# Eight of twelve slices of the modulation matmul are computed inside the prompt's attention; the attention's order of work is changed; pads move the rings in SBUF

## The reference

```python
mod = silu(c) @ w_mod + b_mod            # (1024) @ (1024 x 6144), per sequence
sh1, sc1, gt1, sh2, sc2, gt2 = split(mod, 6)
h = x * (1 + sc1) + sh1
x = LN1(ALPHA * x + (1 + gt1) * mixer(h))   # h @ w_in, attention A and B, RMS norms, @ w_out
h = x * (1 + sc2) + sh2
x = LN2(ALPHA * x + (1 + gt2) * PEER(h))    # 8 heads, top 16 of 128 x 128 experts each
```

## Time and profile before

| | us |
|---|---|
| median of three runs | 4421.73 (4414.55 to 4424.63) |
| the profiled execution, its own time | 4414.03 |
| its span | 4412.2 |
| PE busy | 3550.2, 80% |
| DVE busy | 3054.6, 69% |
| POOL busy | 2662.0, 60% |
| ACT busy | 793.1, 18% |
| mean granted clock of PE | 0.907 of full |

### The profile page before, as it was taken

One profiled execution on the slowest core, in us unless ns is written; L12 is line 12 of the kernel. 1 busy time (PEld: TensorE's weight loads), 2 busy tenths in 40 slices (PEclk: granted clock), 3 DMA queues, 4 the chain that ended last, 5 costly groups with the idle time before them and its releaser, 6 DMA issues. The chain is left out here.

```text
span 4412.2 us, 36769 instructions
## 1 busy us (share of the span) xinstructions
PE 3550.2 (80%) x10274; PEld 1775.6 (40%) x10274; DVE 3054.6 (69%) x7027; ACT 793.1 (18%) x1597; POOL 2662.0 (60%) x2632
## 2 busy tenths in 40 slices
PE   8885599577777774688888888888888888888887
PEld 1444355354554542333333333343333333333333
DVE  1126777688777875877777777777777777777774
ACT  0141111244444441101101101101111111111100
POOL 0000056465555552777777777777777777777775
PEclk9878799688778887899999999999999999999999
DMA  8320489877777776999999999999999999999998
GB/s 326 114 115 24 157 285 313 316 258 265 258 262 270 274 264 257 388 420 419 416 420 414 413 414 412 416 416 411 411 420 412 414 420 414 411 420 413 411 416 324
DMA packets 436081, 1500.23 MB, mean 340 GB/s; under 512 B 47317, under 2 KB 67797, under 8 KB 433621
## 3 DMA queue, kind: packets, MB, share of 16 engines
q0 software_dynamic: 368640, 1342.34, 77.4%
q1 hardware_dynamic: 51928, 128.60, 7.8%
q10 hardware_dynamic: 15360, 27.53, 1.7%
HBM read 1464.96 MB, written 33.33 MB: 340 GB/s over the span
## 5 line engine op out<-in xcount | busy, mean ns | idle before, releaser
L1679 PE MATMUL e_acc<-e_up,e_diag 128*128 128x512 f32 x4096 | 1951.7, 622 | 330.0 <-DMA e_up<-in_up,e_idx 225.5
L1582 DVE CUSTOM_DVE_ANT_0 e_down<-e_down,e_h_ps 128x1024 f32<-128x1024 f32 x1024 | 1244.0, 1219 | 666.4 <-DMA e_down<-in_down,e_idx 664.6
L1679 PEld LDWEIGHTS e_acc<-e_up,e_diag 128*128 128x128 f32 x4096 | 763.1, 196 | 1478.5 <-issue 821.4
L1509 POOL DMA_INDIRECT e_down<-in_down,e_idx x1024 | 993.6, 970 | 355.5 <-issue 223.3
L1509 POOL DMA_INDIRECT e_up<-in_up,e_idx x1024 | 1001.4, 978 | 332.1 <-issue 271.8
L272 POOL DMA_INDIRECT w_in_a<-in_up,a_idx_up x192 | 220.3, 1147 | 275.5 <-DVE sums L303 216.0
L546 PE MATMUL p_acc<-w_in_a,p_h1t 128*128 128x512 f32 x640 | 282.5, 600 | 45.0 <-DVEq L467 45.0
L1052 PE MATMUL a_turn<-ident_sb,a_prob 128*128 128x128 f32 x784 | 154.6, 340 | 169.7 <-ACT a_prob_t L796 163.2
L303 DVE SCALAR_TENSOR_TENSOR sums<-w_in_a,a_wgt,sums 128x1024 f32<-128x1024 f32 x192 | 263.0, 1370 | 29.8 <-DMA w_in_a<-in_up,a_idx_up 23.2
L1222 ACT ACTIVATE e_gate_e<-e_best,e_neg_b 128x16 f32<-128x16 f32 x64 | 19.7, 307 | 1461.7 <-DVEq L1275 1461.7
L264 POOL DMA_INDIRECT w_in_a<-in_down,a_idx_down x192 | 221.5, 1154 | 79.5 <-issue 50.6
(11 more groups left out here) (206 smaller groups left out, 3471.6 us busy)
## 6 DMA issues: line engine op xcount, KB each, us to landing
wm<-in_w_mod SPq DMA_DIRECT2D x12, 2048.0 KB, 8.7
w_in_a<-in_w_in SPq DMA_DIRECT2D x4, 4096.0 KB, 19.1
e_down<-in_down,e_idx POOLq DMA_INDIRECT x1024, 9.5
e_up<-in_up,e_idx POOLq DMA_INDIRECT x1024, 9.5
w_in_a<-in_w_query SPq DMA_DIRECT2D x1, 8192.0 KB, 28.7
p_xt<-in_x_t SPq DMA_DIRECT2D x10, 512.0 KB, 3.4
scratch_qt<-p_qk_t ACTq DMA_DIRECT2D x10, 512.0 KB, 2.8
a_q_t<-scratch_qt SPq DMA_DIRECT2D x20, 256.0 KB, 6.8
```

What stands on the lines that cost most here:

```text
L1509: pool.indirect_dma_start(ring, None, table, bass.IndirectOffsetOnAxis(ap=index, axis=0)).then_inc(landed, 16)
L1582: nc.vector.tensor_tensor_reduce(row, row, h2_ps[:], 1.0, 0.0, ALU.mult, ALU.add, dots[n % 2][:, s:s + 1]).then_inc(dotted, 1)
L1679: mm = nc.tensor.matmul(acc[t % 2][:, c * 512:(c + 1) * 512], diag[n % 2][:, s, :], up[:, r % RING, c * 512:(c + 1) * 512], start=n % PH = ...
```

## The change

The block `modulation` computes 4 of the 12 slices, those that the projection needs. Its 1 is now added with the bias, in one instruction. SP issues the `w_in` loads right behind the four slices, and the stores of zeros behind these. The other 8 slices are loaded in `attention(0)` into `w_in_a` (free by then), and PE multiplies half a slice (four matmuls) in each of the 16 steps of the first tile. The results lie in the unused halves of the score banks. `mod_rows` is stored in two parts, and the prompt's `rows` are loaded in its second tile.

In both attentions the merge goes behind the head's denominator and side dot rows, the transposes of the merged rows from step 2 to 3, `mix` from steps 3 to 6 to steps 4 to 7, and its two halves have a bank and a wait of their own (`mix_ps`). They are read in steps 7 and 8. In the layer norm two fused instructions take the place of three. ACT does the side rows' `Gelu` ahead of the head's exponential. POOL's `tail` of the sample goes from step 11 to 12, and the transposes of h2 from 12 to 14.

`silu` (64 bytes of a partition) moves into the outer allocation, with a pad of 160 bytes behind it; there are pads of 128 bytes in `projection(1)` and of 32 bytes in `experts`.

```diff
@@ modulation
-    CH, BUFS = 512, 4
-    NCH = 6 * D // CH
+    CH = MOD_CH                      # 512
+    NCH = MOD_FIRST                  # 4; MOD_REST = 8
@@ sync
-            with sp.Fori(1, NCH // BUFS) as r:
-                for b in range(BUFS):
-                    sp.wait_ge(row_done, (r - 1) * BUFS + b + 1)
-                    hold(sp)
-                    sp.dma_start(wm[b][:], ...)
+            w_in = io["w_in"].rearrange("(c p) n -> p c n", p=P)
+            sp.dma_start(keep["w_in_a"][:, :, 0:VA], w_in[:, :, 0:VA]).then_inc(keep["w_in_first"], 16)
+            sp.dma_start(keep["w_in_a"][:, :, VA:], w_in[:, :, VA:2048]).then_inc(keep["w_in_loaded"], 16)
+            sp.dma_start(keep["w_in_b"][:], w_in[:, :, 2048:INW]).then_inc(keep["w_in_loaded"], 16)
             sp.wait_ge(zeroed, 1)
             for slot in (0, 3, 4, 13):
                 sp.dma_start(io["kb"][slot], zeros[:]).then_inc(stored, 16)
                 sp.dma_start(io["vb"][slot], zeros[:]).then_inc(stored, 16)
-            (the three w_in loads)
-            sp.wait_ge(mod_ready, 1)
-            sp.dma_start(io["mod_rows"], mod[:, 2 * D:6 * D]).then_inc(stored, 16)
-            sp.wait_ge(stored, 16 * 9)
+            sp.wait_ge(stored, 16 * 8)
@@ attention
-    M_AT, MIX_AT, READ_AT, LN_AT, H2_AT = 2, (3, 4, 5, 6), 7, 9, 12
+    M_AT, TURN_AT, MIX_AT, READ_AT, LN_AT, TAIL_AT, H2_AT = 2, 3, ((4, 5), (6, 7)), (7, 8), 9, 12, 14
+            mod = sb("mod", [2, 4 * D])
+            wm = [keep["w_in_a"][:, :, b * MOD_CH:(b + 1) * MOD_CH] for b in range(4)]
+        mix_ps = [score[1][:, 512:1024], turn[:, 4:8, :].rearrange("p k q -> p (k q)")]
+            rows_ps = [score[b][0:2, 512:1024] for b in range(2)]
@@ sync, load
+                if not first and not side:
+                    wait(row_added, 2 + ROWS + MOD_REST * 3 // 4)
+                    sp.dma_start(io["mod_rows"][:, 0:3 * D], mod[:, 0:3 * D]).then_inc(mod_stored, 16)
+                    sp.wait_ge(mod_stored, STORES + 16)
+                    load_rows()
...
+                    sp.dma_start(mod[:], io["b_mod"][2 * D:6 * D].partition_broadcast(2)).then_inc(bias_in, 16)
+                    for n in range(4):
+                        load_mod(n)
                 (ln, gn, w_out)
+                    for n in range(4, MOD_REST):
+                        sp.wait_ge(row_done, ROWS + n - 3)
+                        load_mod(n)
@@ vector
             def layer_norm(j):
-                chain.then(nc.vector.tensor_scalar(x2[:], z, mv[:, 0:1], lr[:, 2:3], ALU.subtract, ALU.mult))
-                chain.then(nc.vector.tensor_tensor(x2[:], x2[:], ln[:, 0, :], ALU.mult))
-                nc.vector.tensor_tensor(x2[:], x2[:], ln[:, 1, :], ALU.add).then_inc(x2_ready, 1)
+                chain(nc.vector.scalar_tensor_tensor(out=x2[:], in0=z, scalar=mv[:, 0:1], in1=ln[:, 0, :],
+                                                     op0=ALU.subtract, op1=ALU.mult))
+                ...
+                nc.vector.scalar_tensor_tensor(out=x2[:], in0=x2[:], scalar=lr[:, 2:3], in1=ln[:, 1, :],
+                                               op0=ALU.mult, op1=ALU.add).then_inc(x2_ready, 1)
+            def add_bias(n):
+                at = slice(n * MOD_CH, (n + 1) * MOD_CH)
+                dve.wait_ge(bias_in, SMALL + 16)
+                dve.wait_ge(row_done, ROWS + n + 1)
+                nc.vector.scalar_tensor_tensor(out=mod[:, at], in0=rows_ps[n % 2],
+                                               scalar=0.0 if D <= n * MOD_CH < 2 * D else 1.0,
+                                               in1=mod[:, at], op0=ALU.add, op1=ALU.add).then_inc(row_added, 1)
@@ vector, body
                     mask(i, h)
-                    if not first and h == M_AT:
-                        merge(i - 1)
-                    if not first and h == READ_AT:
-                        mix(i - 1)
+                    if not side and first and h >= 2 and h % 2 == 0:
+                        add_bias(h // 2 - 1)
+                    if not first and h == READ_AT[1]:
+                        read_mix(i - 1, 1)
                     (denominator, dot rows)
+                    if not first and h == M_AT:
+                        merge(i - 1)
                     (weigh, add rows)
+                    if not first and h == READ_AT[0]:
+                        read_mix(i - 1, 0)
+                    if not first and h == READ_AT[1]:
+                        residual(i - 1)
@@ tensor
+            def modulate(n, half):
+                (waits for wm slice n, and for the bank's last reader)
+                for c in range(half * DC // 2, (half + 1) * DC // 2):
+                    mm = nc.tensor.matmul(rows_ps[n % 2], keep["silu"][:, 2 * c:2 * c + 2], wm[n % 4][:, c, :],
+                                          start=(c == 0), stop=(c == DC - 1))
+                if half:
+                    mm.then_inc(row_done, 1)
             (body, after sum_values)
+                    if not side and first:
+                        modulate(h // 2, h % 2)
@@ program
+        keep["silu"] = sb("silu", [P, 2 * DC])
+        sb("line_pad", [P, 40])
```

More of the change, by code:

```diff
@@ L170, in _ @@
             nc.vector.tensor_tensor(silu[:], c_t[:], sig[:], ALU.mult).then_inc(silu_ready, 1)
[L171 to L176 removed]
+            for j in range(NCH):
+                dve.wait_ge(row_done, j + 1)
+                nc.vector.scalar_tensor_tensor(out=mod[:, j * CH:(j + 1) * CH], in0=rows[j % 2][0:2, :],
+                                               scalar=1.0 if j >= NCH // 2 else 0.0,
+                                               in1=bias[:, j * CH:(j + 1) * CH], op0=ALU.add, op1=ALU.add
+                                               ).then_inc(row_copied, 1)
             dve.wait_ge(row_copied, 2 + NCH)
[L178 to L179 removed]
             dve.sem_inc(mod_ready, 1)
@@ L766, in body @@
                             side_rows.take_down(pool, chain, 0, i + 1)
-                    if not first and h == H2_AT - 1:
+                    if not first and h == TAIL_AT:
                         tail(i - 1)
@@ L829, in body @@
                     g = i * HEADS + h
+                    if side and h % 8 == 0 and not (first and h == 0):
+                        side_rows.activate(act, *chunk_before(i, h))
                     act.wait_ge(masked, g + 3)
@@ L848, in body @@
                         square(i - 1)
-                    if not first and h == READ_AT + 1:
+                    if not first and h == READ_AT[1] + 1:
                         root(i - 1)
@@ L945, in weigh_w_out, with read_mix, residual @@
                                         ALU.mult).then_inc(keep["w_out_weighed"], 1)
-            def mix(j):
-                dve.wait_ge(mixed, j + 1)
-                for c in range(2):
-                    chain(nc.vector.tensor_tensor(z[:, c * 512:(c + 1) * 512], score[c][:, 512:1024],
-                                                  rows[:, 0, c * 512:(c + 1) * 512], ALU.mult))
-                chain.wait()
+            def read_mix(j, c):
+                dve.wait_ge(mixed, j * 2 + c + 1)
+                chain.then(nc.vector.tensor_tensor(z[:, c * 512:(c + 1) * 512], mix_ps[c],
+                                                   rows[:, 0, c * 512:(c + 1) * 512], ALU.mult))
                 dve.sem_inc(mix_read, 1)
+            def residual(j):
                 dve.wait_ge(x_sem, (j + 1) * 16)
@@ L1013, in _ @@
             add_rows(0, 8)
-            mix(last)
+            for c in range(2):
+                read_mix(last, c)
+            residual(last)
             add_rows(8, 10)
@@ L1103, in body @@
                     if h + 1 < HEADS:
-                        if not first and h + 1 == BH:
-                            pe.wait_ge(mix_read, i)
+                        if not first and h == BH:
+                            pe.wait_ge(mix_read, i * 2 - 1)
                         scores(i, h + 1)
@@ L1108, in body @@
                         scores(i + 1, 0)
-                    if not first and h == M_AT + 1:
+                    if not first and h == TURN_AT + 1:
                         pe.wait_ge(merged_copied, i)
+                    if not first and h == BH:
+                        pe.wait_ge(mix_read, i * 2)
                     if not first and h == H2_AT + 1:
@@ L1115, in body @@
                         sum_values(*before(i, h, 1))
-                    if not first and h == M_AT:
+                    if not side and first:
+                        modulate(h // 2, h % 2)
+                    if not first and h == TURN_AT:
                         turn_merged(i - 1, g0 + h + 2)
-                    if not first and h in MIX_AT:
-                        mix(i - 1, (h - MIX_AT[0],))
+                    for c in range(2):
+                        if not first and h in MIX_AT[c]:
+                            part = MIX_AT[c].index(h)
+                            mix(i - 1, c, part * DC // 2, (part + 1) * DC // 2)
```

(3 more changed lines are left out.)

117 lines of the change are left out of this document (62 added, 55 removed).

## The result

The changed kernel took 4381.1 us (median of 4 runs, 4377.4 to 4383.7), the kernel before 4418.4 us beside it: a ratio of 0.9924, 95% interval 0.9903 to 0.9944. It is faster by 37 us by the medians, and by 33 by the ratio, where 67 were forecast: the time lies inside the range, but nearer to rival B (4385) than to the forecast (4347). A second set of runs gave 0.9926 (0.9908 to 0.9944). The profiled execution took 4383.3 us, 30.7 less than that of before, and its windows by stage answer to the earlier trace rows.

A forecast was written before the change was run, and what follows sets the result against it. Bounds taken: DMA in experts (2697 of 4412 us), PE in modulation and attention(0)'s first tile (half clock), DVE with its waits in attention(1). -48 + 37 - 8 - 49 = -68 us from 4414.03; forecast 4347, range 4305 to 4390.

The forecast's parts named there:

- rival B: In attention(1) the waits only move: a gain of 1 to 2 us a tile, kernel at 4385; chance 0.14.
- They shrink: Attention(1): DVE's waits for PE, 11.0 us a tile, do not vanish but lose 4.3 through later, split reads.
- I charge nothing more: Attention(1): h2 stores moved to step 15, beside SP's query, mask and x loads, cost nothing beyond the lower bound of 2.
- Modulation, -48 forecast: Front block: four slices instead of twelve, ending near 54.5 us instead of 102.94; gain 48 us, between 44 and 57.
- First tile, +37 forecast: Prompt's first tile in attention(0): eight slices added on PE, 88 us against 51.4; loss 37, between 33 and 41.
- Rival C: Prompt's first tile: the clock does not rise, 164 us instead of 88, kernel at 4426; chance 0.04.
- Second tile and tail, -8 forecast: Attention(0): warm start 3 us, reordered reads and layer norm 3, tail 2; gain 8, bounds 3 and 13.
- the tile starts at full clock, so I take 3 us: Attention(0)'s second tile: full clock instead of half for two or three heads, ACT's chain covering part; gain 3 us.
- Attention(1), -49 forecast: Seven reordered tiles: 8.8 us a tile by terms, taken as 7; gain 49 us, bounds 14 and 84.
- The waits for the root and in `weigh` go: Attention(1): DVE's waits for the square root, 1.4 us a tile, and of `weigh`, 2.3, go through the new order.
- Pads, 0 forecast: Rings put on 256-byte boundaries: experts unchanged, having that already; attention(1) 0 us, bounds 0 and 2.
- The rows show half a per cent between the two stages: Pads: 413 GB/s off a boundary in attention(1) against 415 on one in experts, set against up to 6% by the skill.

The follow-up runs named there:

- h2 at 13, second sum: Changed kernel with h2 turned at step 13, first four slices asked for ahead of k_t, last Gelu ahead of last squares on ACT: 4354.8 us, 0.9877.
- h2 at 12, first sum: Changed kernel with h2 at step 12, early slices, and in attention(1)'s end Gelu ahead of squares, four rows added before the merge: 4369.9 us, 0.9905.

## Why the prediction was wrong, and where it was right

The gain was forecast at 67 us and is 33 to 37. The step that failed is that of `attention(1)`, -49 forecast and -22.2 measured: "They shrink", of the waits for PE (11.0 to 6.7 us a tile forecast, 10.9 measured), the waits for ACT that were to go and stayed at 3.8, and "I charge nothing more" for the moved h2 stores, which cost 17.6 us after the last tile. Next comes the second tile of `attention(0)` (-8 forecast, +3.6 measured). With the first tile 5.6 us over its term and `modulation` 4.9 us better than its own, the terms miss by 39 us together, and by 27 of them in one stage. That the time still fell into the range is due to the width of the range.

**Modulation, -48 forecast, -52.9 measured.** Right in mechanism, mis-sized by the rate: 17.8 MB at 408 GB/s with 3 us ahead and 3 behind is 50, the number that the prediction worked out and passed over.

**First tile, +37 forecast, +42.6 measured** (134.63 to 228.41, and 0.2 us at the stage's start). Two terms were too small, by little each. A half slice takes 3.53 us from its first matmul to the next instruction (151.86 to 155.39) where 3.43 was taken, and a head's other matmuls 1.71 in the mean where half of the old head, 1.61, was taken: the shapes of the score, the turn and the values fall from 1.65, 0.90 and 1.49 us to 0.91, 0.55 and 0.83 between the two clocks, which is 0.55 to 0.61 and not 0.5. Over fifteen heads that is 3.0 us. The first head costs 2.7 more, mostly the stall of 5.42 us where 3 stood; asking for the slices first took it down to 2.70. Rival C (clock at 1.2 GHz through the tile) did not come: 1.00 from 189.8 to 228.4.

**Second tile and tail, -8 forecast, +3.6 measured** (120.6 us from 228.41, 117.0 from 238.54). The step "the tile starts at full clock, so I take 3 us" failed in its sign. What is late next is ACT's chain, it doesn't get faster, and a faster PE only waits longer for it and loses its clock. DVE's masks of heads 1, 8 and 15 of that tile, us from the start of the stage, show what each part did:

```
                            head 1   to head 8   to head 15   to the end
before                        59.2        38.8         21.9         54.5
old order, split, pads       101.5        41.6         22.9         53.7
new order, slices in front    59.2        36.4         25.8         57.8
changed                      101.1        36.1         25.8         57.7
changed, h2 at 12            101.2        36.1         28.9         51.8
```

With the old order the split makes the heads up to 8 slower by 2.8 us; with the new one it makes no difference (36.4 and 36.1), and they are 2.7 faster than before. The heads behind them are 3.9 slower in the new order, where second read, residual and layer norm stand in a row on DVE. h2 at 14 costs 5.9 in the tail against 12, and saves 3.1 ahead of it.

**Attention(1), -49 forecast, -22.2 measured.** Three steps, each with its ledger over seven tiles:

- *"The waits for PE shrink"* from 11.0 to 6.7 us a tile. They stayed at 10.9. The three stalls that the prediction wrote down as 2.4, 1.9 and 2.1 are five; the waits of one tile of the changed kernel, DVE's timeline:

```profile
1119.95 0.62 DVE L941 CUSTOM_DVE_ANT_0 a_prob<-a_score,a_mask_b,a_neg_sink 128x384 f32<-128x384 f32 x1 [2.50 <-PE a_score L1091]
...
1127.75 0.62 DVE L941 CUSTOM_DVE_ANT_0 a_prob<-a_score,a_mask_b,a_neg_sink 128x384 f32<-128x384 f32 x1 [2.11 <-PE a_score L1091]
...
1133.18 0.62 DVE L941 CUSTOM_DVE_ANT_0 a_prob<-a_score,a_mask_b,a_neg_sink 128x384 f32<-128x384 f32 x1 [2.21 <-PE a_score L1091]
...
1144.15 0.69 DVE L975 TENSOR_TENSOR a_merged<-a_turn,a_rows 128x512 f32<-128x512 f32 x1 [3.00 <-PE a_turn L1133]
```

  With 0.44 at the mask of head 8 they are 10.3 us; in the tile before they were 4.8, 2.0 and 3.9, 10.7. The same sum in more pieces. While the projection runs, PE is the slower of the two (5.4 us a head warm, more while cold, against 4.9), and where DVE puts its reads doesn't shorten PE. Leaving out half of the matmuls took 53 us of the waits away.
- *"The waits for the root and in `weigh` go"*, 3.7 us a tile. They are 3.8. The prediction counted the wait for ACT's place in the head, but not what the moved h2 puts before it: copy, scaling and three issues, from 1611.9 to 1615.8 behind the last tile, one step ahead of the Gelu. With h2 at 12 or 13 these waits are gone.
- *"I charge nothing more"* for the moved stores. They cost 17.6 us after the last tile (24.66 less 7.11), 13.1 of it one landing behind a load of 5 MB. The prediction named SP's loads of query, mask and x beside the stores, and not this one.

What the steady tiles did gain, 4.5 us each, is the rows' waits (4.4 to 0.3) and 0.7 of layer norm (1.28 and 1.32 us for the passes in the earlier trace rows). The forecast had the layer norm and no term for the rows. Across all variants of the loop the waits change places:

```
us over seven tiles           for PE   for rows   for ACT     sum
before                          77.0       30.8      25.9    133.7
old order, split, pads          78.8       26.4      21.2    126.4
changed (h2 at 14)              76.1        2.0      26.4    104.5
h2 at 13                        97.1        1.3       0       98.4
h2 at 13, second sum            91.5        2.3       0       93.8
the same, load behind stores    96.9        2.0       0.3     99.2
h2 at 12                        77.1       19.9       0       97.0
h2 at 12, first sum             73.2       37.9       0      111.1
h2 at 12, stores at 15          77.5       27.2       0      104.7
h2 at 12, half the matmuls      24.4       37.5       0       61.9
```

So rival B, whose mechanism this is, describes the result better than the forecast did; I had given it 0.14. That its time (4385) is so near is in part luck: it gave `attention(1)` 10 us where 22.2 came, and the second tile a gain of 8 where 3.6 were lost. Why the gathered rows are late with h2 at 12 and not at 13 stays open in part. With h2 at 13 DVE is held for PE at head 15, just ahead of where it waits for rows otherwise, which speaks for its pace; the stores in flight are not excluded, and POOL's place in its queue was not tried.

**Pads, 0 forecast.** The number was right against the kernel before, whose experts' ring stood on a boundary, and the reason was not. "The rows show half a per cent between the two stages" compared 25 us of attention(1), in which 2.8 of the 10.3 MB were not gathered rows, with 2000 us of `experts`. The same 2000 us of `experts`, with the ring on its boundary and off it, are at 415 GB/s and at 405 and 406. The pads kept 61 us that `silu` would have cost. The Trainium skill (DMA: Bandwidth & Descriptors, How a descriptor splits into AXI transactions) says that a transaction must start at a 256-byte boundary, and that a transfer which does not start on one begins with a transaction from the boundary below it. For a 4096-byte row that makes 17 transactions for 16, from which the prediction worked out its estimate of 6%. The runs agree in that rows off the boundary cost time where the DMA engines are full, and not in the 6%: the stage is 2.2% longer, at 64 and at 128 bytes.

## What to carry to other kernels

Before you credit a reordering with the waits that it moves, compare the two engines' work head by head in that stretch: if the other one is slower there, the wait stays and only its place changes. When a store moves later, look up who rewrites its source and which bulk load stands before it in the queues; one wait that holds the load back made the wait behind the store 10.8 us shorter. And when a tensor is added anywhere, work out anew where the rings of the DMA-bound stage start: 64 bytes cost 61 us here.

## What the hardware showed that I had not expected

- Gathered 4096-byte rows into a ring off a 256-byte boundary cost 59 to 61 us in 2697 where the DMA share is 1.01 (399 GB/s for 408), equally at 64 and 128 bytes past it, and nothing that could be told (887.3 and 885.4 us) in `attention(1)` at a share of 0.77.
- Handing PE a warm clock ahead of a chain on ACT gave nothing: 4.86 us of idle time, and the granted clock is 0.50 again. With the same order the heads up to 8 take 36.1 us entered at full clock and 36.4 entered at 0.50.
- A store of 512 KB beside gathers lands in 18.4 us with 5 MB issued 4.4 us ahead of it on another engine's queue, and in 9.2 with that load held back until the stores had landed (10.6 in the kernel before).
